# Retention's input projection as transposed products of halved blocks, with the gates moved to the closing product

## The reference

```python
def retention_layer(x, g_pre, w_in, gn_gain, w_out, g_post):
    proj = rmsnorm(x, g_pre) @ w_in            # 1024 x 6144
    q, k, v, gate = split(proj)
    q, k = rope(q), rope(k) * RET_QK_DIM ** -0.5
    # per head: inner = (q k^T * decay) v; cross = q R * xi; R = R * g_c + (k * zeta)^T v
    o = normalize(inner + cross) * gn_gain     # over the 256 columns of a head
    y = (silu(gate) * o) @ w_out               # 2048 x 1024
    return x + rmsnorm(y, g_post)
```

## Time and profile before

| | |
|---|---|
| median of 3 runs | 2459.2 us (2458.67 to 2461.54) |
| the profiled execution, its span | 2458.8 us |
| PE busy | 2428.7 us, 99% |
| DVE, ACT, POOL busy | 1442.4, 983.5, 669.2 us |
| retention's projections end, first closing steps end | near 630, 673.9 us |

### The profile page before, as it was taken

One profiled execution on the slowest core, in us unless ns is written; L12 is line 12 of the kernel. 1 busy time (PEld: TensorE's weight loads), 2 busy tenths in 40 slices (PEclk: granted clock), 3 DMA queues, 4 the chain that ended last, 5 costly groups with the idle time before them and its releaser, 6 DMA issues.

```text
span 2458.8 us, 34179 instructions
## 1 busy us (share of the span) xinstructions
PE 2428.7 (99%) x11952; PEld 2045.9 (83%) x11952; DVE 1442.4 (59%) x2622; ACT 983.5 (40%) x1861; POOL 669.2 (27%) x1006
## 2 busy tenths in 40 slices
PE   8999999999999999999999999999999999999998
PEld 6888888888888998888888888888887888888887
DVE  4563543635532431277765687787559766787785
ACT  5443433433412432555554553454333233333332
POOL 3453443534200220622221011011124233333112
PEclk9999999999999999999999999999999999999999
DMA  6230211202532322222225201102432434663432
GB/s 220 71 90 19 80 56 37 87 21 75 184 118 88 117 66 84 68 63 62 89 102 176 70 27 49 63 28 80 131 133 108 182 113 171 244 242 127 166 96 85
DMA packets 93761, 251.23 MB, mean 102 GB/s; under 512 B 10225, under 2 KB 31089, under 8 KB 92785
## 3 DMA queue, kind: packets, MB, share of 16 engines
q1 hardware_dynamic: 93616, 249.31, 29.8%
HBM read 181.12 MB, written 63.96 MB: 100 GB/s over the span
## 4 chain that ended last, share of the span: by engine, by line
PE 90%; DVE 4%; issue 2%; ACT 2%; DMA 1%; SPq 0%; POOL 0%; DVEq 0%; ACTq 0%; POOLq 0%
PE ra_qkv_ps L1255 14%; PE ff_ps L4058 11%; PE ff_ps L4085 11%; PE gl_vr_ps L2689 7%; PE ra_gate_ps L1255 7%; PE wa_y_ps L375 6%; PE wb_y_ps L3046 4%; PE la_x_ps L1488 4%; PE wc_y_ps L3427 3%; PE gl_j_ps L2648 3%; PE ff_ps L4116 2%; PE la_cq_ps L1410 1%; PE la_kv_ps L1410 1%; PE gl_l_ps L2715 1%; PE at_T_ps L1980 1%
## 5 line engine op out<-in xcount | busy, mean ns | idle before, releaser
L4085 PE MATMUL ff_ps<-ff_p,ff_p 128*128 128x512 f32 x1176 | 267.7, 389 | 0.3 <-DVE ff_odd L3945 0.3
L4085 PEld LDWEIGHTS ff_ps<-ff_p,ff_p 128*128 128x128 f32 x1176 | 220.5, 188 | 47.4 <-issue 1.1
L1040 DVE TENSOR_TENSOR ra_sT<-ra_s_ps,ra_decay 128x128 f32<-128x128 f32 x64 | 18.6, 291 | 188.5 <-PE ra_s_ps L1294 188.5
L3704 ACT ACTIVATE ff_p<-ff_h 128x1024 fp32r<-128x1024 f32 x51 | 54.2, 1062 | 162.6 <-PE ff_ps L4085 162.6
L1255 PE MATMUL ra_qkv_ps<-ra_wide_h,ra_xl 128*128 128x512 f32 x256 | 104.1, 406 | 8.7 <-DVE ra_wide_l L985 8.4
L883 POOL TENSOR_TENSOR ra_rot<-ra_qk,ra_cos 128x128 f32<-128x128 f32 x64 | 32.0, 499 | 294.0 <-ACT ra_qk L675 294.0
L2416 POOL TENSOR_SCALAR gl_mo<-gl_so 128x1 f32<-128x1 f32 x32 | 17.0, 530 | 332.3 <-ACT gl_osq L2354 332.3
L3929 DVE TENSOR_TENSOR ff_p<-ff_h,ff_p 128x1024 fp32r<-128x1024 f32 x51 | 80.7, 1582 | 42.7 <-ACT ff_p L3704 42.7
L1255 PE MATMUL ra_qkv_ps<-ra_narrow_h,ra_xl 128*128 128x512 f32 x256 | 103.7, 405 | 0.0
L375 PE MATMUL wa_y_ps<-wa_wh,wa_gl 128*128 128x512 f32 x256 | 102.3, 400 | 0.8 <-DVE ra_vl L1060 0.6
L2689 PE MATMUL gl_vr_ps<-gl_vrh,x_lower 128*128 128x512 f32 x256 | 102.1, 399 | 0.0
(11 more groups left out here) (524 smaller groups left out, 7309.7 us busy)
## 6 DMA issues: line engine op xcount, KB each, us to landing
ff_h<-hidden SPq DMA_DIRECT2D x53, 512.0 KB, 3.4
hidden<-ff_s SPq DMA_DIRECT2D x29, 512.0 KB, 2.8
ff_v<-in_w_ff SPq DMA_DIRECT2D x28, 512.0 KB, 6.9
ra_raw<-in_w_wide_a SPq DMA_DIRECT2D x24, 512.0 KB, 3.9
ff_b<-in_w_ff SPq DMA_DIRECT2D x24, 512.0 KB, 6.1
hidden<-ff_a SPq DMA_DIRECT2D x24, 512.0 KB, 2.7
ra_raw<-in_w_narrow_a SPq DMA_DIRECT2D x16, 512.0 KB, 3.9
staging<-in_w_vr_c SPq DMA_DIRECT2D x16, 512.0 KB, 4.4
```

Of the source, the lines that this page charges most:

```text
L3704: act.activation(slots[n % 3][0][:, :, :], h_raw[n % 4][:, :, :], ACT.Copy).then_inc(ph_done, 1)
L4085: end = pe.matmul(to[:, u, :], a[:, k, i * P:(i + 1) * P], b[:, k, :], start=(opens and p < 3 and k == 0 and m == 0), stop=(k == 1 and m = ...
```

## The change

**Projection.** The 6144 columns become 12 chunks of 512: four of gates, then eight heads (q and k by rotation halves, and v). Each chunk's product of 1024x512 weights and 1024x1024 tokens is cut into halves both ways and made of seven products (Winograd's form), each 24 matmuls of 128x512 with the weights stationary: 12 x 7 x 24 = 2016. The output is transposed: columns on partitions, tokens along the row. Token factors (x11, x12, s3, s2, s1, x22, s4) are formed at the start by ACT, DVE and POOL, weight factors for every chunk by four POOL sums (t1 to t4), and split by ACT (`w_upper`) and DVE (`w_lower`), two products ahead, in a ring of three. ACT's `snap` and DVE's `add` put a chunk's four quarters together. The first products run in the order `FIRST` gives, chunks 0 and 1 interleaved.

**1/rms and gates.** Tokens now lie along the row, so the 1024 values of 1/rms go to DRAM (`scale_a`), come back broadcast to all partitions (512 KB), and POOL multiplies gates and rotation tables by them. ACT applies Silu and the group-norm gain to the gates, which go to DRAM (`silu_a`).

**Core.** POOL rotates a head's halves in pieces of 128x512 and 128x1024, and the head is stored (`heads_a`) and reread a chunk later as tiles of 128x4x128. A step has three transposes (a head's last step two) instead of two; the core of a head runs in the slots of the next chunk (14 slots, two per product), the last head's in the slots of the closing product. The stored tile is normalized but not gated.

**Closing product.** DVE multiplies the transposed values by the stored gates (`product`), ACT splits off the upper part, and POOL (was DVE) the lower. `w_out` loses the gain, and POOL forms ten of its sixteen rows' lower parts. Later stages keep their work.

```diff
-                hi, lo = weights
-                for kt in rows:
-                    if first_at is not None:
-                        pe.wait_ge(inl_done, first_at + kt + 1)
-                    for i, (a, b) in enumerate(((tokl, hi), (tokh, lo), (tokh, hi))):
-                        last = pe.matmul(out, a[:, kt, t * P:(t + 1) * P], b[:, kt, at:at + HALF],
-                                         start=(kt == 0 and i == 0), stop=(kt == KT - 1 and i == 2))
-                return last
...
+        X_FACTORS = (a11, a12, s3, s2, s1, a22, s4)
...
+        FIRST = [(0, 0), (1, 0), (0, 1), (1, 1)] + [(c, p) for c in range(2) for p in range(2, PRODUCTS)]
+        FIRST += [(c, p) for c in range(2, CHUNKS) for p in range(PRODUCTS)]
+        PLACE = {key: n for n, key in enumerate(FIRST)}
...
+            return (s[B11], s[B21], s[B12], t2, t1, s[B21], s[B22])[p]
...
+        SCORES_AT = {3: 0, 4: 1, 6: 2, 7: 3, 9: 4, 10: 5, 12: 6, 13: 7}
+        ATTEND_AT = {5: 0, 6: 1, 8: 2, 9: 3, 11: 4, 12: 5, 14: 6, 15: 7}
+        NORM_LATER = 4
...
+        EARLY = {(FINAL, 10): (0, 0), (FINAL, 12): (0, 1), (CHUNKS, 0): (1, 0), (CHUNKS, 1): (0, 2), (CHUNKS, 2): (1, 1),
+                 (CHUNKS, 3): (1, 2), (CHUNKS, 9): (0, 3), (CHUNKS, 11): (1, 3)}
...
+        ROWS_AT = {(FINAL, 7): 0, (FINAL, 9): 1, (FINAL, 11): 2, (FINAL, 13): 3, (CHUNKS, 0): 4, (CHUNKS, 1): 5, (CHUNKS, 3): 6,
+                   (CHUNKS, 5): 7, (CHUNKS, 6): 8, (CHUNKS, 7): 9, (CHUNKS, 8): 10, (CHUNKS, 9): 11, (CHUNKS, 10): 12,
+                   (CHUNKS, 11): 13, (CHUNKS, 12): 14, (CHUNKS, 13): 15}
+        POOL_ROWS = (0, 1, 2, 3, 4, 6, 8, 10, 12, 14)
...
         def row_upper(act, kt):
+            act.wait_ge(row_in[ROW_FROM[kt]], 16 * row_use(kt))
+            if kt < 8:
+                act.wait_ge(f_mm, 2 * PLACE[FINAL, 2 + kt // 2] + 2)
...
+        def product(dve, t, q):
...
+            dve.tensor_tensor(gates_of(t, q), g_bank(t, q)[:, :].rearrange("p (k n) -> p k n", k=4), gates_of(t, q),
+                              ALU.mult).then_inc(prod_done, 1)
...
+            sp.wait_ge(xrms_done, NT)
+            with nc.allow_non_contiguous_dma("one value of each token"):
+                sp.dma_start(scale_a.rearrange("a (t p) -> p (a t)", p=P), xrms[:, 1, :]).then_inc(scale_out, 16)
+            sp.wait_ge(scale_out, 16)
+            sp.dma_start(rms_row[:, :], scale_a[0, :].partition_broadcast(P)).then_inc(scale_in, 16)
...
+            for kt in (10, 11, 12, 13):
+                load_row(kt)
+            store_output(h, 2)
+            load_row(14)
...
+            def w_upper(n):
+                c, p = FIRST[n]
+                factor_ready(act, c, p)
+                if n >= 3:
+                    act.wait_ge(f_mm, 2 * (n - 3) + 2)
+                act.activation(ring[n % 3][0][:, :, :], factor(c, p)[:, :, :], ACT.Copy).then_inc(wh_done, 1)
+            def snap(c, p, j):
+                place_of = {0: C11, 3: C21, 4: C22, 6: C12}[p]
+                act.wait_ge(f_mm, 2 * PLACE[c, p] + j + 1)
+                if c and j == 0:
+                    act.wait_ge(c_out[place_of], stored(place_of, c))
+                act.activation(formed[place_of][:, j, :], chain(c)[:, j, :], ACT.Copy).then_inc(snap_done, 1)
...
+            GATES_STEPS = {(0, 6): ((0, 0), (0, 1)), (1, 2): ((0, 2),), (1, 3): ((0, 3),), (1, 5): ((1, 0),), (1, 6): ((1, 1),),
+                           (2, 0): ((1, 2),), (2, 1): ((1, 3),), (2, 4): ((2, 0),), (2, 6): ((2, 1),), (3, 0): ((2, 2),),
+                           (3, 1): ((2, 3),), (3, 4): ((3, 0),), (3, 6): ((3, 1),), (4, 0): ((3, 2),), (4, 1): ((3, 3),)}
+            SQUARES = {5: (0, 1), 6: (2, 3, 4), 7: (5, 6), 8: (7,)}
+            for n, (c, p) in enumerate(FIRST):
+                if n + 2 < len(FIRST):
+                    w_upper(n + 2)
+                for j in range(2):
+                    slot = 2 * p + j
+                    if p in (3, 4, 6) or p == 0 and c != 1:
+                        snap(c, p, j)
+                    if (c, p) == (1, 2):
+                        snap(c, 0, j)
...
+                for t in SQUARES.get(n, ()):
+                    square_x(t)
+                for cc, order in GATES_STEPS.get((c, p), ()):
+                    gates(cc, order)
...
+            def scale_gates(c, order):
...
+                dst = formed[place_of][:, :, :]
+                pool.tensor_tensor(dst, dst, rms_row[:, half * HALF:(half + 1) * HALF].rearrange("p (a n) -> p a n", a=1)
+                                   .broadcast_to([P, 2, HALF]), ALU.mult).then_inc(gm_done, 1)
...
+            def rotate(h, half):
...
+                x_ = formed[place_of]
+                pool.tensor_tensor(turned[:, 0, :], x_[:, 1, :], sin[:, at], ALU.mult)
+                pool.tensor_tensor(turned[:, 1, :], x_[:, 0, :], sin[:, at], ALU.mult).then_inc(turn_part, 1)
+                pool.wait_ge(turn_part, 3 * n + 1)
+                pool.tensor_tensor(x_[:, :, :], x_[:, :, :], cos[:, at].rearrange("p (a n) -> p a n", a=1).broadcast_to([P, 2, HALF]),
+                                   ALU.mult).then_inc(turn_part, 1)
+                pool.wait_ge(turn_part, 3 * n + 2)
+                pool.tensor_tensor(x_[:, 0, :], x_[:, 0, :], turned[:, 0, :], ALU.subtract).then_inc(turn_part, 1)
+                pool.tensor_tensor(x_[:, 1, :], x_[:, 1, :], turned[:, 1, :], ALU.add).then_inc(turn_done, 1)
...
+            for t in range(4):
+                deviation(h - 1, t)
+                row_lower(pool, t, rows_l_pool)
+            deviation(h - 1, 4)
+            g_lower(pool, 0, 0)
+            g_lower(pool, 0, 1)
+            rotate(h, 1)
+            deviation(h - 1, 5)
...
+            def w_lower(n):
+                c, p = FIRST[n]
+                dve.wait_ge(wh_done, n + 1)
+                upper, lower = ring[n % 3]
+                dve.tensor_tensor(lower[:, :, :], factor(c, p)[:, :, :], upper[:, :, :].bitcast(F32), ALU.subtract).then_inc(wl_done, 1)
...
+            for n, (c, p) in enumerate(FIRST):
+                if n + 2 < len(FIRST):
+                    w_lower(n + 2)
...
+                if n == 1:
+                    scale_rows(x21, 0, x21_in)
+                    dve.wait_ge(xg_pool, 1)
+                    dve.wait_ge(xg_dve, 1)
+                    dve.tensor_tensor(s3_sum, x11[:, :, :], x21[:, :, :], ALU.subtract).then_inc(xs_done, 1)
+                    form_lower(s3, s3_sum, 9)
+                if n == 2:
+                    scale_rows(x22, 1, x22_in)
+                    form_lower(a22, x22[:, :, :], 10)
+                if n == 3:
+                    dve.wait_ge(xg_dve, 2)
+                    dve.wait_ge(xl_set, 10)
+                    dve.tensor_tensor(x22[:, :, :], x21[:, :, :], x22[:, :, :], ALU.add).then_inc(xs_done, 1)
+                    dve.wait_ge(xs_done, 2)
+                    dve.tensor_tensor(x11[:, :, :], x22[:, :, :], x11[:, :, :], ALU.subtract).then_inc(xs_done, 1)
+                    form_lower(s2, x11[:, :, :], 11)
+                if n == 4:
+                    form_lower(s1, x22[:, :, :], 12)
...
+                elif p in (3, 4, 6):
+                    pe.wait_ge(snap_done, 8 * c + {3: 0, 4: 2, 6: 4}[p] + j + 1)
...
+            def project(c, p, j):
+                n = PLACE[c, p]
+                upper, lower = ring[n % 3]
+                xh_, xl_ = X_FACTORS[p]
+                to = chain(c) if p in (0, 3, 4, 6) else apart(c, p)
+                if j == 0:
+                    pe.wait_ge(wl_done, n + 1)
+                bank_ready(c, p, j)
+                for kt in range(KT // 2):
+                    if j == 0:
+                        x_ready(c, p, kt)
+                    for i, (a, b) in enumerate(((lower, xh_), (upper, xl_), (upper, xh_))):
+                        last = pe.matmul(to[:, j, :], a[:, kt, j * P:(j + 1) * P], b[:, kt, :],
+                                         start=(p < 3 and kt == 0 and i == 0), stop=(kt == KT // 2 - 1 and i == 2),
+                                         skip_group_check=p > 2)
+                last.then_inc(f_mm, 1)
```

1713 lines of the change are left out of this document (941 added, 772 removed).

## The result

| | before | after |
|---|---|---|
| median | 2460.18 us (2458.67 to 2461.54, 4 runs) | 2577.25 us (2572.66 to 2579.79, 4 runs) |
| ratio | | 1.0477, 95% interval 1.0462 to 1.0492 |
| span of the profiled execution | 2458.8 us | 2578.0 us |

A forecast was written before the change was run, and what follows sets the result against it. The prediction took TensorE, busy 2428.7 of 2458.8 us, as the bound: 2458.8 - 61.8 + 3.6 + 20 + 18.5 + 6 + 26 = 2471.1, forecast 2471 us, 0.5% slower. Its own range was 2455 to 2486, with rivals 2438 to 2496.

The forecast's parts named there:

- Start, +3.6: Program start: first matmul at 12.0 instead of 8.41, waiting for x and the split weights; +3.6 us, bounds 2 to 6.
- Forming, +20: Forming token factors in the first nine products: PE waits for DVE, slowed by POOL; +20 us, 9 to 28.
- turns: DVE and POOL operations with two SBUF operands wait for each other; about 2.4 us for each of DVE's first five steps.
- Row of 1/rms, +18.5: Before product (1,3): PE waits while 1/rms goes to DRAM and back, store taken as 4 us; +18.5 us, 11 to 24.
- bound of 8: Store of 1/rms: up to 8 us if each of 1024 elements costs a packet of the mean time, 0.125 us.
- third rival: Store of 1/rms as single numbers is slow, 14 us instead of 4: +10, 2481 us; chance 0.07.
- Steady chunks, +6: Gate chunks 38.3 us, head chunks PE's 49.7 plus 0.75 for DVE's waits; +6 us, 0 to 30.
- second rival: Head chunks bound by DVE and POOL: mean wait 0.4 us over 31 operations, 52.5 a chunk, 2487 us; chance 0.17.
- Tail, +26: Start of the closing product: PE waits for w_out rows, gated values, a normalization and tile 0's finish; +26 us, 16 to 36.
- -61.8: PE's work: 2016 instead of 2304 projection matmuls saves 65.7 us, 56 more transposes cost 3.9; net -61.8 us.
- The clock, priced at 4 us in all: Slower matmuls after PE's long waits in forming and before (1,3), at the lower clock level: 2 us a time.
- faster rival: DVE and POOL do not meet, as in the feed-forward stage: 24 us less in forming, chunks and tail, 2447; chance 0.30.

The follow-up runs named there:

- e1: Changed kernel with GpSimd's rotation of q and k left out but for 8 of 512 columns: 2534.71 us, 43 less.
- e4: Changed kernel with GpSimd's four sums and cosine product, 128x1024, each split into two of 128x512, same arithmetic: 2550.5 us, ratio to before 1.0377.
- e6: Changed kernel with DVE's lower parts of the weights in head chunks cut to 8 of 256 columns, GpSimd in full: 2546.38 us.
- e5: Changed kernel with GpSimd's rotation cut to 8 of 512 columns and its head-chunk weight sums to 8 of 256: 2516.06 us, 61 less.
- e9: Changed kernel with twelve extra matmuls that nobody reads ahead of the waiting matmul at six head-chunk borders: 2564.42 us, ratio to before 1.0442.
- e11: Changed kernel with the post gain's load moved ahead of SP's six last stores of head 7's tiles: 2575.7 us, ratio to before 1.0484.
- e10: Changed kernel with second and later loads of w_out rows into each of four slots left out, values wrong: 2564.91 us, ratio to before 1.0432.
- e12: Changed kernel with early 1/rms squares, GpSimd's wide operations halved, twelve extra matmuls per border and earlier post gain load: 2529.12 us, ratio to before 1.0294.

## Why the prediction was wrong in size
By its own steps:

- **Start, +3.6:** right. The first matmul ran at 11.89 instead of 8.41.
- **Forming, +20:** nearly. (0,2) at 41.90 (42), (0,3) at 58.94 (62 to 65), then a wait of 3.90 at 76.13 that wasn't foreseen; (0,6) ended at 88.9 instead of 84, some 5 us of the term. The turns of the earlier trace rows are the mechanism, as said.
- **Row of 1/rms, +18.5:** the round that PE waits for is right, the store mis-sized. 11.2 us instead of 4; the excess over the prediction's bound of 8 is 3 us. The stall was 22.07 instead of 16.5. The third rival had the cause right. The Trainium skill ("DMA: Bandwidth & Descriptors", "Rules for kernel authors") names a strided last dimension as one descriptor per element; the trace agrees: some 1040 packets of 4 bytes start between 92.4 and 93.1. But the packets are not what takes the time, as the bound of 8 had it: the DMA engines' busy share from 92 to 103 is 0.04, and the store lands some 9 us behind the last packet. What these 9 us are stays open. With another wait of 2.5 us at 132.44, chunk 2 began at 143.4, where the steps so far gave 130.
- **Steady chunks, +6: this is the step that failed.** Seven head chunks take 60.6 us in the mean (424 from 259 to 683), where 49.7 + 0.75 was forecast: 71 us of the 107 that the sum was short. The gate chunks were right (38.1 for 38.3). The size of the turns was nearly right too: from the groups above, eight ra_ql, eight ra_sTl, seven ra_Rl and eight normalizations a chunk are longer by 0.49, 0.42, 0.46 and 0.32 us, and five lower parts of weights by 0.34 (1563 ns against 1220): 15 us over 36 operations, 0.41 us each. That is the 0.4 of the second rival. Even DVE's busy sum came out: 40 us and 31 turns of 0.3 are 49.3, and a middle chunk has 49.4. But the forecast's 49.7 + 0.75 and that rival's 52.5 fail by the same step: both set DVE's *busy sum* against PE's, as if DVE could work all the time. It can't work ahead. It waits for ACT's upper part of the state, ACT for DVE's update, PE for ACT's copy, and the stretched operations stand in that round. So DVE idles 11.5 us of a middle chunk of 60.9; in e1, e4 and e6 it is busy for 41.4, 46.7 and 43.7 us and idles 13.4, 10.2 and 12.3. e5 shows what stretches the round: without GpSimd's wide operations a middle chunk is 50.7 us and PE doesn't wait in it.
- **What the 71 us are made of.** 60 of them go with GpSimd's wide operations (the mean of the seven is 60.6, and 52.0 in e5). The other 11 lie in the last of the seven, in e5 as well (61.6 against 50.7): ACT's wait for a row of `w_out`, and the slow matmuls behind it. The prediction had nothing there. Of the chunk whose window stands under e1, 60.55 us, PE idles 5.9 and is busy for 54.6, 3.9 more than e5's 50.7, at a granted clock of 0.95; e9 gave 2.3 of that back. PE's own work was right: 49.7 and eight third transposes of 0.07, which the 49.7 leaves out, are 50.3.
- **Tail, +26:** some 53, of 39 and 14. The listed waits came where they were forecast, at 7.88, 5.32, 5.43, 8.23 and 6.48 us instead of 7.5 to 8, 1.8, 2.5, 7 and 2; with three smaller ones they sum to 39 instead of 26.8. Row 8's load, the normalization and the finish were priced as if their queues were empty; e11 and e10 show SP's queue and the rows' slots in them. The other 14 us or so are the lower clock in that stretch, 0.83, an estimate from the paces in the next point. (Start, chunks and tail were short by 13, 71 and 27, 111 in all; the 4 above 107 are the third transposes, which the sum has in its -61.8.)
- **The clock, priced at 4 us in all:** from the timeline's pace (start to start), matmuls of products cost 0.258 us instead of 0.227 in the first 150 us, 0.244 in the head chunks instead of 0.232 in e5, and 0.296 in the tail instead of 0.2305 before: for 336, 1176 and 192 matmuls 10.5 + 14 + 12.5 = 37 us. Some 2.5 of it the start's slow matmuls cost before as well. With some 12 us by which PE's other work in the seven chunks is longer (377.8 us busy where seven times 50.3 was due, less the 14) that is about the 49 us by which PE's busy time fell short of the forecast fall.
- **"Seven-product work runs beside POOL's sums and PE doesn't wait"**, the ground of the faster rival, was the wrong comparison. The feed-forward stage has no recurrence; here one passes from DVE through ACT to PE in every step.

The Trainium skill ("SBUF — State Buffer", section "SBUF: two separate sides") has it that the shared port pair is held for a whole instruction. e4 agrees: with the same work on GpSimd in halves, DVE's longest operations got shorter, and 27 us came back. The prediction quoted the rule and then took the turns as a sum on DVE's row, as if no other engine waited for that row.

What stays open: which of the tail's chains would be the last one with the others gone, why the row of `w_out` lands late in the last head chunk, and whether another order of the border (ACT's copy first) would hide the turns.

## What to carry to other kernels
Where an engine's operations are links of a round trip (state, upper part, copy, matmul), price a slow-down of each on the round trip, not on that engine's busy total. Here 0.4 us an operation made a middle chunk 10 us longer, while DVE's busy sum of 49.4 us would still have fitted beside PE's 50.7. Put short operations on GpSimd beside such a chain, or none. And where the granted clock falls behind a wait on TensorE, price the wait twice: the wait, and the slower matmuls behind it.

## What the runs showed of the hardware
- An operation with one tensor operand in SBUF waits as well: the normalization, a TENSOR_SCALAR of 128x256, took 718 ns in the mean beside GpSimd, 395 without; the longest shown took 1.94 us and ended 0.15 us after GpSimd's 2.46. The prediction had counted only those with two.
- Even a step of one column on GpSimd is stretched: L1151 (128x1) took 1.05 us in the mean in the head chunks, against the 0.57 of the earlier trace rows; the one at 341.26, which meets VectorE's lower part of the weights, takes 1.49.
- The store of 1024 single numbers took 11.2 us from issue to landing, though its packets all start within 0.7 us.
- Behind the wait of 3.9 us at a head chunk's border the granted clock is at the lower level (0.50 from 501 to 506; 0.95 in the mean of a chunk). With 2.7 us of matmuls whose results nobody reads put into the wait, the chunk's is 1.00 and the kernel is 13 us shorter; beside the halves (e12) they gained nothing.
